# GpSimd updates half of the residual at the ends of post-norm stages

## The reference

```
for i in range(DEPTH):
    ff = swiglu(rms_norm_2(h, g[0]), ffn_w_gate_up[i, 0], ffn_w_down[i, 0])
    h = h + 0.5 * rms_norm_2(ff, g[1])
    mix = short_conv_mixer(rms_norm_2(h, g[2]), ...)    # layer 0; layer 1: gated_deltanet_mixer
    h = h + rms_norm_2(mix, g[3])
    ff = swiglu(rms_norm_2(h, g[4]), ffn_w_gate_up[i, 1], ffn_w_down[i, 1])
    h = h + 0.5 * rms_norm_2(ff, g[5])
```

## Time and profile before

| | us |
|---|---|
| median of 3 runs | 1993.9 |
| lowest, highest run | 1991.03, 1994.35 |
| profiled execution, first to last instruction (span) | 1991.5 |
| TensorE busy | 1961.4 (98%) |
| VectorE busy | 1398.7 (70%) |
| ScalarE busy | 1095.4 (55%) |
| GpSimd busy | 125.0 (6%) |

### The profile page before, as it was taken

How to read it: one execution, slowest core, us unless ns; L and a number is a source line. 1 busy time by engine, 2 the same in 40 slices (tenths; PEclk the granted TensorE clock), 3 DMA queues, 4 the chain that set the end, 5 groups by cost and what they waited for, 6 DMA issues and landing times.

```text
span 1991.5 us, 41716 instructions
## 1 busy us (share of the span) xinstructions
PE 1961.4 (98%) x15682; PEld 1827.6 (92%) x15682; DVE 1398.7 (70%) x2392; ACT 1095.4 (55%) x1828; POOL 125.0 (6%) x204
## 2 busy tenths in 40 slices
PE   9999999999999999999999999999999899999998
PEld 7999999989999999999999999999999899989997
DVE  6687877766788877666667766666658977577655
ACT  5665555556654655554454544454447777565443
POOL 2031000000040000000000000000000432000000
PEclk9999999999999999999999999999999899999999
DMA  9433665554335555465546465555554535455552
GB/s 319 143 128 128 217 210 189 187 170 149 128 118 190 200 187 186 156 212 189 190 159 212 151 202 187 189 174 187 188 190 150 164 123 155 149 173 195 188 187 82
DMA packets 117817, 348.51 MB, mean 175 GB/s; under 512 B 23288, under 2 KB 35912, under 8 KB 117184
## 3 DMA queue, kind: packets, MB, share of 16 engines
q1 hardware_dynamic: 114960, 335.23, 50.6%
q0 software_dynamic: 2736, 11.59, 1.7%
HBM read 340.81 MB, written 5.96 MB: 174 GB/s over the span
## 4 chain that ended last, share of the span: by engine, by line
PE 90%; DVE 4%; ACT 2%; issue 1%; DMA 1%; POOL 1%; SPq 0%; DVEq 0%; ACTq 0%; POOLq 0%
PE bank L2317 28%; PE bank L2319 27%; PE bank L2318 27%; PE bank L2609 1%; ACT whi L991 1%; DVE arena L1576 1%; DVE wlo L1537 1%; DVE conv L2038 1%; PE bank L2353 1%; PE bank L2582 0%; DMA relay<-arena 0%; PE bank L2796 0%; PE bank L2570 0%; PE bank L2362 0%; DVE xlo L1548 0%
## 5 line engine op out<-in xcount | busy, mean ns | idle before, releaser
L2317 PE MATMUL bank<-xhi,whi 128*128 128x256 f32 x3368 | 958.4, 285 | 7.3 <-DVE arena L2031 2.6
L2318 PE MATMUL bank<-xlo,whi 128*128 128x256 f32 x3368 | 943.9, 280 | 1.1 <-issue 1.1
L2319 PE MATMUL bank<-xhi,wlo 128*128 128x256 f32 x3368 | 943.2, 280 | 1.1 <-issue 1.1
L1537 DVE TENSOR_TENSOR wlo<-raw,whi 128x1024 fp32r<-128x1024 f32 x621 | 750.1, 1230 | 199.6 <-ACT whi L991 196.9
L2317 PEld LDWEIGHTS bank<-xhi,whi 128*128 128x128 f32 x3368 | 635.7, 189 | 24.3 <-issue 6.1
L2318 PEld LDWEIGHTS bank<-xlo,whi 128*128 128x128 f32 x3368 | 636.2, 189 | 5.8
L991 ACT ACTIVATE whi<-raw 128x1024 fp32r<-128x1024 f32 x621 | 632.2, 1045 | 11.9 <-DMA raw<-panels 6.2
L2319 PEld LDWEIGHTS bank<-xhi,wlo 128*128 128x128 f32 x3368 | 635.8, 189 | 1.2 <-issue 1.2
L2317 PE MATMUL bank<-whi,hhi 128*128 128x512 f32 x688 | 272.8, 396 | 0.0
L2319 PE MATMUL bank<-whi,hlo 128*128 128x512 f32 x688 | 271.2, 394 | 0.0
L2318 PE MATMUL bank<-wlo,hhi 128*128 128x512 f32 x688 | 270.4, 393 | 0.0
(11 more groups left out here) (376 smaller groups left out, 1751.8 us busy)
## 6 DMA issues: line engine op xcount, KB each, us to landing
raw<-panels SPq DMA_DIRECT2D x621, 512.0 KB, 3.8
arena<-w_in POOLq DMA_DIRECT2D x2, 2048.0 KB, 10.5
arena<-relay SPq DMA_DIRECT2D x8, 512.0 KB, 5.0
arena<-gains_in POOLq DMA_DIRECT2D x6, 512.0 KB, 3.9
relay<-arena POOLq DMA_DIRECT2D x4, 512.0 KB, 9.1
relay<-arena SPq DMA_DIRECT2D x4, 512.0 KB, 3.6
x<-x_in SPq DMA_DIRECT2D x1, 1024.0 KB, 5.0
arena<-bias_table POOLq DMA_DIRECT2D x8, 128.0 KB, 6.5
```

The source lines that it names most:

```text
L1537: dve.tensor_tensor(wlo[slot][:], raw[slot][:], whi[slot][:].bitcast(F32), ALU.subtract) \
L2317: pe.matmul(dst, w_hi, a_hi, start=start, stop=False, skip_group_check=True)
L2318: pe.matmul(dst, w_hi, a_lo, start=False, stop=False, skip_group_check=True)
L2319: return pe.matmul(dst, w_lo, a_hi, start=False, stop=stop, skip_group_check=True)
```

## The change

At the five ends the update of quarters 0 and 1 goes from VectorE to GpSimd, in two operations each: `gained` times `post_rstd` in place (tensor_scalar), and x plus that (tensor_tensor), with a wait on a new semaphore `gained_scaled` between them. GpSimd starts when `post_rstd` is there, when quarters 0 and 1 of `gained` are written, when TensorE has read them and the old x (`x_turned`, third group), and when VectorE has updated quarters 2 and 3. VectorE makes all eight `xlo` one after another. The last stage's end is as before. Apart from this, the semaphores `table_product` and `table` of the bias table become one that counts to two.

```diff
@@ GpSimd
-                    pool.wait_ge(y["table"], 1)
+                    pool.wait_ge(y["table"], 2)
...
+            def update_first_half(s):
+
+                if s + 1 == n_stages:
+                    return
+                n = posts_before(s)
+                pool.wait_ge(post_rstd_ready, 3 * n + 1)
+                pool.wait_ge(post_gained, QUARTERS * n + CHUNKS)
+                pool.wait_ge(x_turned, len(TURNS) * (s + 1) + 3)
+                pool.wait_ge(x_updated, QUARTERS * s + CHUNKS)
+                for q in range(CHUNKS):
+                    pool.tensor_scalar(gained[:, q, :], gained[:, q, :], post_rstd[:, q:q + 1], None, ALU.mult)                         .then_inc(gained_scaled, 1)
+                    pool.wait_ge(gained_scaled, CHUNKS * n + q + 1)
+                    pool.tensor_tensor(x_quarter(q), x_quarter(q), gained[:, q, :], ALU.add).then_inc(x_updated, 1)
...
                     if post_norm(s):
                         load_gain(s)
+                        update_first_half(s)
...
                 load_gain(s)
+                update_first_half(s)
@@ VectorE, finish(s)
                     update(2)
                     update(3)
-                    for k in range(KT // 2):
+                    for k in range(KT):
                         prepare_tile(s + 1, k)
-                    update(0)
-                    for k in range(KT // 2, KT):
-                        prepare_tile(s + 1, k)
-                    update(1)
                     prepare_rstd(s + 1)
                     return
@@ VectorE and TensorE, bias table
-                            dve.wait_ge(y["table_product"], 1)
+                            dve.wait_ge(y["table"], 1)
...
-                                .then_inc(y["table_product"], 1)
+                                .then_inc(y["table"], 1)
...
-                            pe.wait_ge(y["table"], 1)
+                            pe.wait_ge(y["table"], 2)
```

More of the change, by code:

```diff
@@ L548, in build @@
         y = {name: sem("y_" + name) for name in (
-            "consts table_product table stored rel_loaded small_loaded tile_read tok_read "
+            "consts table stored rel_loaded small_loaded tile_read tok_read "
             "gla_gained squared qk_ms qk_root qk_scaled qk_turned nsa_ready moba_ready gains low_tanh gsum cmp_x "
@@ L581, in build @@
         post_gained = sem("post_gained")
+        gained_scaled = sem("gained_scaled")
         post_sum_ready = sem("post_sum_ready")
```

## The result

The changed kernel takes 1997.65 us (median of 9 runs, 1996.54 to 2002.04), the kernel before 1993.9 (9 runs, 1989.88 to 1995.54). The ratio is 1.0027, with a 95% interval of 1.0019 to 1.0035: slower by 0.27%, some 5 us. (The ratio takes in all runs; the means differ by 5.2 us, the two medians by 3.75.) I had forecast 1991.6, no measurable change, on the fast side of it. The change is small but real, and it goes the other way: it is rival C, GpSimd as the bound. The profiled execution has a span of 1995.2 us, against 1991.5.

A forecast was written before the change was run, and what follows sets the result against it. TensorE, busy 98% of the span, was taken as the bound. Four ends at -0.49 and DELTA at -0.34 summed to -2.3 us, taking 1993.9 to 1991.6, no measurable change; range 1988.0 to 2000.0.

The forecast's parts named there:

- rival C: At the stage ends GpSimd becomes the bound: over 4 us slower from d = 0.92 on, e.g. 1999.3 us; chance 0.18.
- The gain at `xlo`: Without VectorE's two updates, xlo 4 to 7 come earlier, so TensorE's second panel can gain 0.65 us per end.
- the late chain: Quarter 1's update, ScalarE's second square, root, VectorE's reciprocal, weight low half, then TensorE's third panel; 0.15 us to spare.
- d: Shift of the late chain when GpSimd finishes quarter 1, T - 4.60: forecast -0.34 us, between -0.96 and +3.42.
- VectorE's longer wait: VectorE's wait for the root grows from 1.54 by 1.5 us plus d; nothing later falls behind.
- D: Rival: GpSimd's reads stretch VectorE's xlo low halves, +3.3 us, 1997.2; chance 0.07 together with anything unforeseen.
- T: Time from GpSimd's start at a stage end until quarter 1 is done: forecast 4.26 us, between 3.64 and 8.02.
- my own rule: Third panel shifts by max(-0.65, d - 0.15) at four ends, by d at DELTA; forecast sum -2.3 us.
- rival B: GpSimd's operations moderately slow, T from 4.7 to 5.5: e.g. +2.2 us, 1996.1, no measurable change; chance 0.18.
- A tensor_scalar over 1.1 us: Sign named beforehand: such a GpSimd row would make the sum wrong in size and probably in sign.
- the bound: 1.77 from above: Upper limit for GpSimd's unmeasured tensor_scalar, from the slower two-operand mean; lower limit the memset's 0.54; 0.8 taken.
- the conversion: GpSimd's one-input conversion, 2.102 us for twice the elements, taken as 1.05 for this shape when pricing the tensor_scalar.

The follow-up runs named there:

- e6: Changed kernel plus 27 lone GpSimd operations behind the last update of x, to price each; kernel time means nothing, tensor_scalar of 128x512 took 1.56 us.
- e5: Changed kernel plus a spare 0.74 us two-operand VectorE operation between xlo 3 and xlo 4; ratio 1.0042 to the kernel before.
- e2: Changed kernel, but GpSimd scales gained into two spare buffers as soon as post_rstd is there, only the additions waiting; ratio 0.9991 to the kernel before.
- e1: Changed kernel, but GpSimd scales gained by a tensor_tensor with post_rstd broadcast instead of a tensor_scalar; ratio 0.9995 to the kernel before.

## Why the prediction was wrong

Most steps held. The gain at `xlo` was 0.66 of the predicted 0.65 (all five ends), the wait that bounds the third panel is the late chain, its slack is 0.12 where I had 0.15, and DELTA shifts by d itself (1.04 for d = 1.05). VectorE's longer wait, the later load of the gain and the table cost nothing that shows, and `xlo` was not disturbed (2.44 for six, 0.41 each): D is out. DELTA's shift holds at the wait; beyond it the stage's own scatter hides it.

The step that failed is a term of T: "I take 0.8, midway between memset and conversion", for the tensor_scalar. It takes 1.56, twice per end: + 1.52. The tensor_tensor takes 1.09 for my 1.25 (- 0.32). GpSimd starts 0.2 later than I let it: 0.27 after the last thing it waited for, where ScalarE starts 0.04 after the same products (1319.68). With these, T = 5.45 and d = (1319.91 - 2.16) + 5.45 - 1322.15 = 1.05, and my own rule gives 4 x (1.05 - 0.15) + 1.05 = +4.65 us, against 4.8 read from the trace. So the mechanism was right and a size off, and the size decided the sign, at T = 4.72, as the text said. By its lateness this is rival C (d from 0.92 on); a T of 5.45 with the start that I had assumed gives d = 0.85 and +3.7 us, still rival B. That the time falls between 1988.0 and 2000.0 is no merit of the sum, since the range was drawn to take in C. A tensor_scalar over 1.1 us was named beforehand as the sign that the sum would be wrong in size and probably in sign, and so it was.

I had the bound: 1.77 from above. Where I went wrong is in reading the conversion, at 1.05, as a ceiling of sorts for a one-input operation. That left the 1.56 outside the forecast. The GPSIMD Engine Reference of the Trainium skill (section 4.1, Engine selection) has one-input work at roughly line-rate; the copy in e6, 0.61 beside the memset's 0.54, agrees, and the tensor_scalar, one-input too, does not. The measurement decides. The conversion itself was no firm row either: it took 2.10 in the profile before and 1.17 in the one after.

Section 8 (Key points) of the same page of the Trainium skill has GpSimd contend with VectorE instructions that read two SBUF inputs or run in a 2-port mode. The traces agree for two inputs: in e5 GpSimd's operation grew from 1.09 to 1.48. In e2 VectorE's diagonals, with one matrix input, grew from 0.48 to 0.91; in which mode they ran no run shows.

## What to carry to other kernels

When a step is moved to a slower engine, follow the last of its results to who waits for it, and price the chain to TensorE in slack: here 0.12 us of slack stood against 1.05 us of lateness, and a gain of 0.66 ahead of it was worth nothing. For an operation that no row shows, work out the value at which the sign turns first, and spread the chances over both sides of it unless a row of that very kind says otherwise. Look for idle time of the same engine between the instructions that matter before calling on another one: 0.78 us of VectorE's own held the 0.74 us update.

## What the runs showed of the hardware that I had not expected

- On GpSimd a tensor_scalar of 128x512 f32 takes 1.56 us, and a tensor_tensor with the same column broadcast 1.04 (e6). Doing this one-input product as a two-input one saves a third.
- GpSimd took 0.27 us from the modelled end of TensorE's products to its first tensor_scalar (1319.64 to 1319.91), and 0.25 to its first tensor_tensor (e1), ScalarE 0.04. The trace does not say what the 0.27 is made of.
- In e2 two short VectorE tensor_scalars (128x128) went from 0.48 to 0.91 beside a GpSimd tensor_scalar. VectorE's two-operand updates behind them kept their time beside the same GpSimd operation, and the next one, which started while they ran, grew by 0.41. What decides which side pays was not settled.
